# A two-block transformer kernel: where the input rows and the arena begin in a partition of SBUF

## The reference, cut to what matters

```
first stack, per layer:
  x = layer_norm(A*x + 0.5*swiglu(x, ffn_w_in[0], ffn_w_out[0]))   # 1024 -> 2*2816 -> 1024
  x = layer_norm(A*x + token_mix(x))       # stick-breaking attention, gated delta rule, short conv
  x = layer_norm(A*x + 0.5*swiglu(x, ffn_w_in[1], ffn_w_out[1]))
  x = layer_norm(A*x + sigmoid(x @ gate + b) * (p @ proj))
second stack, per layer:
  h = x @ w_in                             # MLA and differential attention, gates
  y = gated attention branches; merged = g0*(y_a @ wa) + g1*(y_b @ wb)
  x = layer_norm(A*x + merged @ w_out)
```

## Time and profile before

| | |
|---|---|
| median of three runs | 1547.9 us (1547.41 to 1548.25) |
| the profiled execution: its own time | 1548.5 us |
| its span, first to last instruction | 1546.6 us |
| mean granted clock of TensorE | 0.998 of full |
| TensorE busy, matmuls | 1530.1 us (99%), 13300 |
| TensorE busy, weight loads | 1481.8 us (96%), 13300 |
| GpSimd / ScalarE / VectorE busy | 1236.2 / 882.5 / 772.7 us |
| the 16 DMA engines | 47% of the span, 167 GB/s |

### The profile page before, as it was taken

The page is one execution under the profiler, slowest core; times in us unless marked ns, Lnnn a source line. Parts: engine busy times, 40 slices in busy tenths (PEclk is TensorE's granted clock), DMA queues, the critical chain, the costliest instruction groups (busy, mean ns, idle before and its releaser), DMA issues.

```text
span 1546.6 us, 32926 instructions
## 1 busy us (share of the span) xinstructions
PE 1530.1 (99%) x13300; PEld 1481.8 (96%) x13300; DVE 772.7 (50%) x1524; ACT 882.5 (57%) x1231; POOL 1236.2 (80%) x970
## 2 busy tenths in 40 slices
PE   8999999999999999999999999999999999999997
PEld 8999999999999999999999999999998999989997
DVE  4222179758222285221488574211676664666555
ACT  5434487467434486344585575344677565766653
POOL 8988878458999878988788189988878667887675
PEclk9999999999999999999999999999999999999999
DMA  7655544324555545555544145555545434553331
GB/s 302 214 192 184 186 166 150 111 83 164 209 200 191 190 165 176 196 187 190 188 140 164 57 150 178 191 191 191 187 141 188 139 137 146 186 189 138 137 137 55
DMA packets 36707, 258.53 MB, mean 167 GB/s; under 512 B 4064, under 2 KB 4320, under 8 KB 5984
## 3 DMA queue, kind: packets, MB, share of 16 engines
q1 hardware_dynamic: 35712, 254.30, 46.5%
q10 hardware_dynamic: 864, 2.28, 0.4%
HBM read 255.52 MB, written 1.05 MB: 166 GB/s over the span
## 4 chain that ended last, share of the span: by engine, by line
PE 94%; DVE 3%; ACT 1%; DMA 0%; issue 0%; POOL 0%; ACTq 0%; SPq 0%; DVEq 0%
PE psum L802 25%; PE psum L804 24%; PE psum L803 24%; PE psum L790 3%; PE psum L785 3%; PE psum L786 3%; PE psum L1098 2%; PE psum L1346 1%; PE psum L958 1%; PE psum L1357 1%; PE psum L1375 1%; ACT wh L1489 0%; PE psum L1366 0%; DVE arena L2045 0%; PE psum L1302 0%; DVE psum L2060 0%
## 5 line engine op out<-in xcount | busy, mean ns | idle before, releaser
L1446 POOL TENSOR_TENSOR wl<-raw,wh 128x512 fp32r<-128x512 f32 x960 | 1231.9, 1319 | 293.6 <-ACT wh L1489 286.3
L802 PE MATMUL psum<-xs,wh 128*128 128x256 f32 (+1 forms) x1984 | 565.2, 285 | 0.6 <-DVE psum L2505 0.6
L804 PE MATMUL psum<-xs,wl 128*128 128x256 f32 (+1 forms) x1984 | 555.7, 280 | 0.0
L803 PE MATMUL psum<-xs,wh 128*128 128x256 f32 (+1 forms) x1984 | 555.4, 280 | 0.0
L1489 ACT ACTIVATE wh<-raw 128x2048 fp32r<-128x2048 f32 x237 | 453.3, 1914 | 97.8 <-PE psum L804 73.7
L802 PEld LDWEIGHTS psum<-xs,wh 128*128 128x128 f32 x1984 | 373.5, 188 | 8.2 <-issue 4.5
L803 PEld LDWEIGHTS psum<-xs,wh 128*128 128x128 f32 x1984 | 373.9, 188 | 0.8 <-issue 0.5
L804 PEld LDWEIGHTS psum<-xs,wl 128*128 128x128 f32 x1984 | 373.5, 188 | 0.0
L802 PE MATMUL psum<-arena_r,wh 128*128 128x256 f32 x1168 | 327.5, 280 | 0.0
L803 PE MATMUL psum<-arena_r,wh 128*128 128x256 f32 x1168 | 326.6, 280 | 0.0
L804 PE MATMUL psum<-arena_r,wl 128*128 128x256 f32 x1168 | 326.0, 279 | 0.0
(11 more groups left out here) (341 smaller groups left out, 1828.1 us busy)
## 6 DMA issues: line engine op xcount, KB each, us to landing
raw<-wstream SPq DMA_DIRECT2D x238, 1024.0 KB, 4.8
cst<-consts SPq DMA_DIRECT2D x1, 1541.5 KB, 13.8
raw<-wstream SPq DMA_DIRECT2D x3, 512.0 KB, 8.2
out<-xT SPq DMA_DIRECT2D x4, 256.0 KB, 2.6
sm<-small ACTq DMA_DIRECT2D x2, 455.5 KB, 5.3
xT<-xt ACTq DMA_DIRECT2D x1, 768.0 KB, 7.0
raw<-wstream SPq DMA_DIRECT2D x2, 256.0 KB, 5.2
sm<-small ACTq DMA_DIRECT2D x2, 147.0 KB, 4.7
```

What stands on the lines that cost most here:

```text
L802: mm(o, a[0], b[0], start=start, stop=False, skip_group_check=shared)
L803: mm(o, a[0], b[1], start=False, stop=False, skip_group_check=shared)
L804: return mm(o, a[1], b[0], start=False, stop=stop, skip_group_check=shared)
L1446: return nc.gpsimd.tensor_tensor(wl[:, s, quarter(q)], raw[:, s, quarter(q)], wh[:, s, quarter(q)].bitcast(F32), ALU.subtract)
```

## The change

`tiny` shrinks from 256 to 216 elements (`hb` moves inside it), which puts `arena` at byte 119,552 and `xs` at 210,688, both multiples of 256. `xs` becomes [128, 8, 576]: a block is still 2304 bytes (nine times 256), but `X_AT` now gives the high and the low row of a block their own offsets, in elements. A small class `Split` makes the slices.

```diff
-X_ROW = 288
-X_AT = {(-1, 3): 28, (0, 0): 30, (0, 1): 4, (0, 2): 8, (0, 3): 12, (1, 0): 20, (1, 1): 8, (1, 2): 28, (1, 3): 0, (2, 4): 2}
+X_BLOCK = 576
+X_AT = {(-1, 3): (0, 288), (0, 0): (0, 316), (0, 1): (0, 272), (0, 2): (0, 288), (0, 3): (0, 304), (1, 0): (0, 258), (1, 1): (16, 304), (1, 2): (0, 272), (1, 3): (12, 300), (2, 4): (0, 268)}
...
-        tiny = sb("tiny", [P, 256])
+        tiny = sb("tiny", [P, 216])
         A_SIZE = 22784
...
-        xs_rows = sbr("xs", [P, KD, 2, X_ROW])
+        xs_rows = sbr("xs", [P, KD, X_BLOCK])
+
+        class Split:
+            def __init__(self, at, width):
+                self.at, self.width = at, width
+
+            def __getitem__(self, key):
+                rows, k, half, cols = key
+                first, last, _ = cols.indices(self.width)
+                return xs_rows[rows, k, self.at[half] + first:self.at[half] + last]

         def x_from(li, s):
-            return xs_rows[:, :, :, X_AT[li, s]:X_AT[li, s] + S + 2]
+            return Split(X_AT[li, s], S + 2)

         def x_of(li, s):
-            return x_from(li, s)[:, :, :, 0:S]
+            return Split(X_AT[li, s], S)
...
-        hb = tiny[:, 208:224]
+        hb = tiny[:, 136:152]
...
-                src = unnormed(at, s)[:, :, :, 0:S + 2]
+                src, cols = unnormed(at, s), slice(0, S + 2)
...
-                        m = by_high(o[b][:, 0:S + 2], w.take(1, t + LEADS * k + b), pair(src, k), k == 0, False)
+                        m = by_high(o[b][:, 0:S + 2], w.take(1, t + LEADS * k + b), pair(src, k, cols), k == 0, False)
...
-                        m = by_low(o[b][:, 0:S + 2], w.take(1, t + LEADS * k + b), pair(src, k), k == KD - 1, False)
+                        m = by_low(o[b][:, 0:S + 2], w.take(1, t + LEADS * k + b), pair(src, k, cols), k == KD - 1, False)
...
-                src = unnormed(li, 2)[:, :, :, 0:S + 2]
+                src, cols = unnormed(li, 2), slice(0, S + 2)
...
-                        m = mm3(o[:, 0:S + 2], w.take(1), pair(src, k), k == 0, k == KD - 1)
+                        m = mm3(o[:, 0:S + 2], w.take(1), pair(src, k, cols), k == 0, k == KD - 1)
```

## The result

The changed kernel takes 1555.5 us in the median (1555.35 to 1555.83, five runs) against 1547.9 (1547.24 to 1548.25): the ratio is 1.0050 with a 95% interval of 1.0036 to 1.0065. It is slower by 7.6 us, 1.5 us above the upper end of my range. Its span is 1553.7 us instead of 1546.6, with the same instructions, the same granted clock (0.998) and waits no longer than before.

What follows compares the result with a forecast made beforehand. TensorE, busy 99% of the span, was taken as the bound: matmul count times start-to-start distance. The terms by stretch summed to -6.0 us, from the median of 1547.9 to 1542 us; own range 1537 to 1545, over all cases 1532 to 1554.

Steps and rivals of the forecast that it cites:

- The signs that I had named: Arena's six stretches leaving 350 and 353.4 together, or levels below 346 or, for starts on a multiple of 16, above 356.
- What differs between the stretches on xs is where in a partition the moving rows begin: Step tying the xs stretches' pace, 346.5 to 363.3 ns a triple, to the moving rows' start modulo 256.
- The arena (0 / 0): Term for the arena's triples: they stay on 350 or 353.4 ns, so 0 us.
- Block 3 against block 1: 258-column runs: 120.0 ns a matmul starting at a multiple of 256, against 118.6 starting at 192.
- First FFN: Term for 320 triples on xs, rows going to 0 / 128: from 353.5 to 350 ns, -1.1 us.
- The middle level, 350: Pace in ns a triple assumed for xs pairs going to 0 with a low row on a multiple of 16.
- Token mix of layer 0: Term for 144 triples on xs leaving the odd start: from 363.3 to 350 ns, -1.9 us, called the surest.
- Second FFN of layer 0: Term for 288 triples on xs, at the best level before: from 346.5 to 350 ns, +1.0 us.
- First FFN of layer 1: Term for 288 triples on xs, rows going to 0 / 192: from 353.2 to 350 ns, -0.9 us.
- second stack, layer 0: Term for 224 triples on xs, best pair with rows exchanged: from 354.8 to 346.5 ns, -1.9 us.
- Rival C: Starts at a multiple of 256 are bad: 4.2 ns a triple on arena and three FFNs, 1552 us; chance 0.27.
- B: Rival: stretches keep or exchange levels, settled by how each begins; only odd starts gain; 1546.5 us, chance 0.18.

Runs made afterwards that it cites:

- e1: The kernel before with only the arena moved to a multiple of 256, xs keeping its bytes: 1553.5 us, ratio 1.0035.
- e8: The kernel before with nothing moved, but 15 of 16 single weight tiles read from 160 bytes below their place: 1543.7 us in one run.
- e4: The kernel before with only the weights moved up by 96 bytes, arena and xs staying: 1543.7 us, ratio 0.9970.

## Why the prediction was wrong

- *What bounds the kernel, and that nothing hides a change of pace*: right. The view that I took as the decisive one, line 804 by stretch, is where the loss stands. The signs that I had named fired: the arena's six stretches left their two levels together, and the first FFN's 360 is above 356.
- *"What differs between the stretches on xs is where in a partition the moving rows begin"*: this is the step that failed. It is not the start that matters but its distance from the weight tiles, modulo 256. In the kernel before the two can't be told apart, since all weight tiles lie on one byte.
- *"The arena (0 / 0): it sits on 350 or 353.4 now and I let it stay, 0"*: measured +5.6 us, the largest term (e1: the whole kernel +5.3). I carried the levels of one distance, 32, to another, 128, whose level is 356. Block 3 against block 1 of the 258-column rows compared distances 128 and 64 and did say slower by 1.4 ns a matmul. The arena's own comparison gives (356.0 - 351.2) / 3 = 1.6, with the mean over all its triples of before. I had this row and priced a rival with it instead of the forecast.
- *First FFN, 320 x (350 - 353.5) = -1.1*: +2.1 us. "The middle level, 350, for every xs pair that goes to 0" had no row at distance 128 / 0; it is 360.
- *Token mix of layer 0, -1.9*: -1.0. It improved, to 355 and not 350, and leaving the odd start was not needed for it: with that start kept and the weights moved it was at 354.
- *Second FFN of layer 0, +1.0*: +1.9, the direction right; it went to 353.3, not 350.
- *First FFN of layer 1, -0.9, and the last layer, -0.7*: -0.7 and -0.5. Close by luck: they rest on the same middle level, which the first FFN and the second of layer 0 did not have. The token mix of layer 1, put at 0, brought 0.3: my row of before (353.8) was of one piece, and another stood at 367.
- *Second FFN of layer 1, rows exchanged, 0*: 0.0; *second stack, layer 0, the best pair exchanged, -1.9*: -0.3. Exchanging the rows is no symmetry: 48 / 176 at distance gives 346.7 or 353.3, 176 / 48 gives 353.2.
- *`by_input` -0.5*: 0.0. The 258-column products on xs had no term; with the blocks they cost 1.1 us.
- Rival C named the mechanism, the high row's reads against the weight load's at 128 past a multiple of 256, and priced the arena and three FFNs at +8.7 us; measured +5.6, +2.1, +1.9 and -0.7 make +8.9. It missed the time by 3.5 us mainly because it kept my gains of -4.3 us, of which about -1.3 came. That its sum for these stretches came so near is luck in part, since its one price, 4.2 ns a triple, stood for 4.8 on the arena and 6.5, 6.7 and -2.3 on the FFNs. I gave it 0.27. What spoke against it was a comparison of unlike things, 258 columns in the arena with 256 on xs.
- B's "settled by how a stretch begins" is half right: the distance gives the possible levels, and at some distances (192, 208, 48 / 176) there are two, and the way a stretch is entered, or a gap inside it, goes with the change from one to the other. It explains nothing of the change's cost on the arena: at distance 128 all six long stretches run at 356.0 in both traces that have it (the changed kernel and e1), which is above both levels of before.

The Trainium skill's page "TensorE: Matmul & The Clock Gate", section "What happens when you issue a matmul", says that TensorE reads SBUF through two independent ports and that loading the next weights does not take bandwidth from the running matmul. For float32r these runs do not agree. By where the load reads alone, at equal moving rows, a triple takes 342 to 343 ns instead of 350 to 353.3 in the arena's down products, and 358.4 instead of 346.7 in the second FFN of layer 0 (e8 against the kernel before).

Why the level repeats every 256 bytes, why xs and the arena can differ at one distance (360 and 356 at 128), and why there is a lasting second level stay open; no run looked inside.

## What to carry to other kernels

Where TensorE is the bound and every matmul loads new weights, measure the distance from start to start by stretch, and lay the moving rows by their distance from the weight tiles rather than on round addresses. Sweep that distance in one kernel, a value per stage, and then put the best value everywhere, for a stage can have a second level that the sweep does not show. Prefer a value that holds one level in all stretches. Here that was 112 for both rows; no run tells what it is for another type, another number of columns or weights that do not all lie on one byte.

## What the runs showed of the hardware that I had not expected

- With float32r matmuls of 256 columns and new weights for each, the steady pace runs from 113.3 to 122 ns a matmul at full clock, 8% by addresses and state alone. Levels come back to 0.1 ns in different kernels: most are 340.0, 346.7, 350.0, 353.3, 356.0 or 360.0 ns a triple.
- At distance 192 there are two lasting states, 340.0 and 353.3 ns; the pace switched between them at five of eight extra matmuls of 64 columns, and, in e4, behind a single distance of 194 ns.
- Both rows at 112 gave 340 to 341 ns in every long stretch: 1516.1 us against 1548.7 beside it, with only addresses changed.
